# Gates of an RG-LRU recurrence: 64 by 64 quarters of the TensorE array in place of two 128 by 128 products per chunk

## The reference

```
xc = conv_b + causal convolution of xr over 4 tokens          # (T, 512)
xb = xc.reshape(B, T, N_RNN_BLOCKS, RNN_BLOCK)                # 8 blocks of 64 channels
r = sigmoid(einsum('btnc,ncd->btnd', xb, w_a) + b_a)
i = sigmoid(einsum('btnc,ncd->btnd', xb, w_i) + b_i)
log_a = -8 * r * softplus(-lam)
a = exp(log_a)
b = sqrt(-expm1(2 * log_a)) * i * xc
h = scan of  h[t] = a[t] * h[t-1] + b[t]
```

## Time and profile before

| | us |
|---|---|
| runs | 895.73, 898.94, 899.92; median 898.94 |
| profiled execution, its own time | 894.47 |
| its span, first to last instruction | 892.5 |
| TensorE, weight loads, VectorE, ScalarE busy | 861.2, 788.6, 683.0, 574.4 |
| gate stage of layer 0 (first gate product to the next query pair) | 51.79 to 55.98 |
| the same of layer 1 | 384.57 to 388.80 |

### The profile page before, as it was taken

The page is one execution under the profiler, slowest core; times in us unless marked ns, Lnnn a source line. Parts: engine busy times, 40 slices in busy tenths (PEclk is TensorE's granted clock), DMA queues, the critical chain, the costliest instruction groups (busy, mean ns, idle before and its releaser), DMA issues.

```text
span 892.5 us, 15446 instructions
## 1 busy us (share of the span) xinstructions
PE 861.2 (96%) x5827; PEld 788.6 (88%) x5827; DVE 683.0 (77%) x923; ACT 574.4 (64%) x792; POOL 70.8 (8%) x92
## 2 busy tenths in 40 slices
PE   8899999999999999899999999999999999999995
PEld 7856899999999999857899989999998989898994
DVE  5887876666665654877877989789887989789892
ACT  6686755545444534585656777777768777777772
POOL 3540110000000000000231000000000000000000
PEclk9999999999999999999999999999999999999998
DMA  9614034555576753314263999899998999899981
GB/s 312 194 48 144 21 123 147 190 183 188 182 212 183 201 154 107 95 49 142 71 213 118 341 353 371 303 356 400 339 395 295 382 370 363 301 364 391 347 355 26
DMA packets 119004, 208.18 MB, mean 233 GB/s; under 512 B 5920, under 2 KB 71712, under 8 KB 118944
## 3 DMA queue, kind: packets, MB, share of 16 engines
q1 hardware_dynamic: 117232, 201.79, 64.1%
q0 software_dynamic: 1424, 5.24, 2.9%
q10 hardware_dynamic: 288, 0.34, 0.2%
HBM read 202.12 MB, written 5.24 MB: 232 GB/s over the span
## 4 chain that ended last, share of the span: by engine, by line
PE 81%; DVE 10%; issue 3%; DMA 3%; ACT 2%; POOL 0%; ACTq 0%; DVEq 0%; SPq 0%; POOLq 0%
PE ps L2495 20%; PE ps L2520 13%; PE ps L652 11%; PE ps L654 11%; PE ps L653 11%; DVE wlo L1400 5%; PE ps L2097 2%; PE ps L2460 2%; PE ps L2213 1%; DMA raw<-in_moe_w_gate_dram 1%; ACT whi L958 1%; PE ps L2272 1%; DMA raw<-in_moe_w_down_dram 1%; PE ps L2116 1%; PE ps L2507 1%
## 5 line engine op out<-in xcount | busy, mean ns | idle before, releaser
L1400 DVE TENSOR_TENSOR wlo<-raw,whi 128x1536 fp32r<-128x1536 f32 (+4 forms) x298 | 437.8, 1494 | 91.0 <-ACT whi L958 87.8
L958 ACT ACTIVATE whi<-raw 128x1536 fp32r<-128x1536 f32 (+4 forms) x298 | 375.2, 1276 | 142.7 <-PE ps L654 75.6
L652 PE MATMUL ps<-uhi,whi 128*128 128x272 f32 (+1 forms) x576 | 169.2, 294 | 1.3 <-DVE ulo L1423 0.7
L654 PE MATMUL ps<-uhi,wlo 128*128 128x272 f32 (+1 forms) x576 | 165.9, 288 | 0.0
L653 PE MATMUL ps<-ulo,whi 128*128 128x272 f32 (+1 forms) x576 | 165.4, 287 | 0.0
L2495 PE MATMUL ps<-whi,xeh 128*128 128x320 f32 (+1 forms) x512 | 125.7, 326 | 0.0
L2495 PE MATMUL ps<-wlo,xeh 128*128 128x320 f32 (+1 forms) x512 | 124.3, 324 | 0.0
L2495 PE MATMUL ps<-whi,xel 128*128 128x320 f32 (+1 forms) x512 | 124.3, 324 | 0.0
L652 PEld LDWEIGHTS ps<-uhi,whi 128*128 128x128 f32 (+1 forms) x576 | 107.8, 187 | 5.1 <-issue 2.2
L653 PEld LDWEIGHTS ps<-ulo,whi 128*128 128x128 f32 (+1 forms) x576 | 108.0, 188 | 0.5
L654 PEld LDWEIGHTS ps<-uhi,wlo 128*128 128x128 f32 (+1 forms) x576 | 107.8, 187 | 0.0
(11 more groups left out here) (307 smaller groups left out, 1202.4 us busy)
## 6 DMA issues: line engine op xcount, KB each, us to landing
raw<-in_moe_w_down_dram SPq DMA_DIRECT2D x24, 1536.0 KB, 9.0
raw<-in_moe_w_gate_dram SPq DMA_DIRECT2D x16, 1536.0 KB, 7.8
raw<-in_moe_w_up_dram SPq DMA_DIRECT2D x16, 1536.0 KB, 8.3
raw<-in_moe_w_gate_dram SPq DMA_DIRECT2D x16, 1280.0 KB, 9.6
raw<-in_moe_w_up_dram SPq DMA_DIRECT2D x16, 1280.0 KB, 9.1
raw<-in_ffn_w_gate_dram SPq DMA_DIRECT2D x11, 1024.0 KB, 5.1
raw<-in_ffn_w_up_dram SPq DMA_DIRECT2D x11, 1024.0 KB, 5.2
raw<-in_ffn_w_down_dram SPq DMA_DIRECT2D x8, 1408.0 KB, 6.8
```

Of the source, the lines that this page charges most:

```text
L652: pe.matmul(dst, wh, xh, start=start, stop=False, skip_group_check=True)
L654: return pe.matmul(dst, wl, xh, start=False, stop=stop, skip_group_check=True)
L958: act.activation(placed(whi, s, src), src, ACT.Copy).then_inc(hi_done, 1)
L1400: dve.tensor_tensor(placed(wlo, s, src), src, placed(whi, s, src).bitcast(F32), ALU.subtract).then_inc(lo_done, 1)
```

## The change

TensorE works with quarters of its array. For each chunk it takes the two diagonal 64 by 64 matrices of `wa` and of `wi` alone: four products of 64 channels by 272 tokens, where `r` is the half of the channels and `at` the half of the PSUM partitions that takes the result. Half `s = 0` of the channels of both gates goes to the bank of `wa`, half `s = 1` of both to the bank of `wi`. In the first bank gate `wa` has partitions 0 to 63 and gate `wi` 64 to 127, in the second bank they are swapped, so that the four products of a chunk use four different quarters of the array. The list of blocks changes to `wa` 0, `wi` 0, `wa` 1, `wi` 1 and so on, so a chunk has banks 0 and 1 or banks 2 and 3. TensorE waits for both banks of a chunk, and both blocks count as filled together, after the fourth product.

A bank now holds half a chunk of two gates, so ScalarE empties it with two tanhs over 64 partitions, and there are 16 of them per layer. `decay_exp` begins with a new wait of ScalarE for its own mark after the tanhs.

```diff
--- before.py
+++ after.py
@@ -236,8 +236,8 @@
             add("qro", b)
         for j in range(2):
             add("qn", j)
-        for n in ("wa", "wi"):
-            for c in range(CH):
+        for c in range(CH):
+            for n in ("wa", "wi"):
                 add(n, c)
         for j in range(2, NH // 2):
             add("qn", j)
@@ -1079,19 +1079,22 @@
                 pairs("qn", qT, u32, range(2))
 
                 act.wait_ge(hba_done, 1)
-                for name, dst, bias in (("wa", ta, hba), ("wi", tb, hbi)):
-                    for c in range(CH):
-                        b = B[l, name, c]
-                        n = l * CH + c
+                for c in range(CH):
+                    n = l * CH + c
+                    for s, b in enumerate((B[l, "wa", c], B[l, "wi", c])):
+                        r = slice(64 * s, 64 * s + 64)
                         act.wait_ge(filled, b.ready())
-                        act.activation(dst[:, c, :], bank(b), ACT.Tanh, bias=bias[:, n:n + 1], scale=0.5)\
-                           .then_inc(emptied[b.bank], 1)
+                        for kind, (dst, bias) in enumerate(((ta, hba), (tb, hbi))):
+                            at = 64 * (kind ^ s)
+                            q = act.activation(dst[r, c, :], bank(b, slice(at, at + 64)), ACT.Tanh, bias=bias[r, n:n + 1], scale=0.5)
+                        q.then_inc(emptied[b.bank], 1)
                 mark().then_inc(ti_done, 1)
                 act.wait_ge(vec_done, 1)
                 act.wait_ge(xc_done, CH * (l + 1))
 
 
                 def decay_exp():
+                    act.wait_ge(ti_done, l + 1)
                     for c in range(CH):
                         n = l * CH + c
                         act.activation(xr[:, c, 0:T], ta[:, c, :], ACT.Exp, bias=nsp4[:, n:n + 1], scale=nsp4[:, n:n + 1])
@@ -2108,12 +2111,18 @@
                 query_pairs(range(2))
 
                 pe.wait_ge(gdiag_in, 64 * (l + 1))
-                for kind, name in enumerate(("wa", "wi")):
-                    for c in range(CH):
-                        b = B[l, name, c]
+                for c in range(CH):
+                    two = B[l, "wa", c], B[l, "wi", c]
+                    for b in two:
                         fill(pe, b)
-                        pe.wait_ge(xc_done, CH * l + c + 1)
-                        pe.matmul(bank(b), gdiag[:, kind, c, :], xc[:, c, :], start=True, stop=True).then_inc(filled, 1)
+                    pe.wait_ge(xc_done, CH * l + c + 1)
+                    for s, b in enumerate(two):
+                        r = slice(64 * s, 64 * s + 64)
+                        for kind in range(2):
+                            at = 64 * (kind ^ s)
+                            q = pe.matmul(bank(b, slice(at, at + 64)), gdiag[r, kind, c, r], xc[r, c, :], start=True, stop=True,
+                                          skip_group_check=True)
+                    q.then_inc(filled, 2)
                 query_pairs(range(2, NH // 2))
 
                 r = slice(NOPE, QKH)
```

## The result

The changed kernel takes 907.51 us (median of 5 runs, 905.16 to 908.73) against 898.94 (5 runs, 895.73 to 902.68). The ratio is 1.0098, with a 95% interval of 1.0073 to 1.0122: slower, by 8.6 us between the medians. The forecast was 907.2.

A forecast was written before the change was run, and what follows sets the result against it. TensorE and ScalarE were taken to bind side by side, ScalarE with 0.5 us slack. Tanhs +4.43 and wait +0.23, less slack, gave `rr` 4.15 us late per layer, +8.3 on 898.94: 907.2 us, range 901.5 to 911.0.

The forecast's parts named there:

- The step that carried the sum: ScalarE's gate tanhs: no overlap when the first partition changes, 0.50 us apart, run 7.99 us, +4.43 us per layer.
- only the reading side counts: Rival, gate tanhs: only a changed reading partition ends overlap; 3.25 us per layer, 905.4 us; chance 13%.
- the overlap stays: Rival, gate tanhs: starts stay 0.37 us apart; 2.1 us per layer, 903.1 us; chance 14%.
- The added wait: Ahead of decay_exp: waiting for ScalarE's own mark delays the exponentials, +0.23 us per layer.
- The slack: ScalarE up to `rr`: 0.35 us idle at the third key pair plus about 0.15 at `rr`, in all 0.5 us.
- TensorE's place in the wait: At the sums of squares ahead of `rr`: TensorE idles about 1.9 us until ScalarE's mark releases it.
- My 72.44 for L2184: Layer 0, TensorE's sums of squares: start shifts from 68.36 to 72.44 us, released by ScalarE's mark.
- TensorE's saving buys nothing: Gate stage: quarters save TensorE about 2 us, but a wait ahead of `rr` takes its place.
- No slack downstream: Behind `rr`: all is serial, so a late `rr` means a late end, one for one.
- Serial quarters: Rival, TensorE's gates: quarters run one after another, 1.03 us per layer more, 909.3 us; chance 8%.
- The rival that I gave 7%: TensorE's clock drops to half level, costing half of 3.4 us per layer, 910.6 us; chance 7%.

The follow-up runs named there:

- e1: The kernel before with nine groups of 272-column tanhs ahead of ScalarE's first work, differing in height and first partitions read and written; one run, 922.84 us.
- e7: The kernel before with only ScalarE's wait for its mark added ahead of decay_exp; one run, 897.65 us.
- e2: The kernel before with each gate bank emptied by two 64-row tanhs, lower then upper, and the mark's wait added; 903.95 us, ratio 1.0092.
- e4: The changed kernel's TensorE part, blocks and order, but 8 whole 128-row tanhs on ScalarE, mixing the gates' halves; 896.34 us, ratio 0.9989.
- e6: The changed kernel with three more 128 by 128 fp32 products per chunk behind the four quarters; 906.49 us, ratio 1.0084.
- e5: The changed kernel run again unaltered, to see where TensorE's clock falls; 905.94 us, ratio 1.0085.
- e8: The kernel before with squares and copies in pairs() reordered, so the first partition changes 2 times in two blocks instead of 4; one run, 897.49 us.

## Why the prediction was right

- **The overlap.** The step that carried the sum, 0.50 us between starts for every change of the first partition, measured 0.49 to 0.51 in layer 0 and 0.48 to 0.52 in layer 1, and 7.99 us for the run, as forecast. It was an inference from copies that change the reading side only. e1 shows that a change on the writing side (of the output or of the bias column, which moved together) counts too, so "only the reading side counts" and "the overlap stays" are out. The Trainium skill, ScalarE: Activation LUTs, What ACT_TABLE_LOAD costs, has back-to-back activations overlap by about 93 ns. e1 agrees where the first partition stays (0.11 us) and shows none where it changes.
- **The added wait** was put at 0.23 us; the exponentials now start 0.34 us behind the last tanh (61.35 to 61.69) where before they started 0.01 ahead, so 0.35. From mark to next start I took the 0.21 of a copy; to the exponentials it is 0.32 (61.37 to 61.69). In e7, where the mark still overlaps the last whole tanh by 0.1, the exponentials are 0.21 behind it.
- **The slack.** `rr` came 4.19 and 4.13 us late, forecast 4.15 for each. At `rr` the slack was 0.15 us, as I had it: from the root of `ta` to `rr` it is 1.15 us before (69.45 to 70.60) and 1.00 after (74.13 to 75.13). At the third key pair it was more than the idle 0.35 us, as the overlap of 0.11 comes back with it: from the squares ahead to the pair it is 0.76 us before and 0.29 after, 0.47 less. So 4.43 + 0.35 − 0.47 − 0.15 = 4.16. The wait and this slack were both taken 0.12 too small and cancel, which is luck.
- **TensorE's place in the wait** was wrong. I had it idle for 1.9 us at L2184 until ScalarE's mark. It starts L2184 without that, 1.91 us behind the start of the last value blocks (70.92 to 72.83), as in the kernel before (66.45 to 68.36), and waits ahead of these blocks for VectorE's rotation L1511, 0.48 us (1.14 in e2). VectorE works with no pause over 0.04 us from `decay_done`, ScalarE's second mark, up to that rotation, so this path is late together with ScalarE. With 2.24 us from L2184 to `rr` it is ready at 75.07, only 0.06 us before ScalarE. My 72.44 for L2184 (72.78 with the 0.34 us of this execution) hit by another path than the one I gave.
- **TensorE's saving buys nothing.** Shown twice: e4 gives 0.4 to 0.5 us per layer without the doubled tanhs, e6 adds 5.5 us of TensorE and loses 0.4. e2 has none of the saving and the same delay.
- **No slack downstream.** In e2, whose clock fell in the same stage as before's, VectorE's work is 4.3 us late after the gates and `rr` of layer 0 and 8.7 after those of layer 1, of which 0.2 and 0.3 came in ahead of the gates. Nothing was absorbed.
- **Serial quarters** are out: eight passes start within 0.30 us. The Trainium skill's sentence on four independent tiles (TensorEngine Tiling (Array Packing), Tiling Modes) holds here for fp32 and for both row groups.
- **The clock** fell in both gate stages of both profiles of the changed kernel; in the first, TensorE was at work for 1.51 of the 4 us ahead. The rival that I gave 7%, a fall ahead of L2184 at 1.7 us per layer, came in neither. A fall in the gates I had called hidden, without a chance for it: three of the four were, as ScalarE had more to do than TensorE even at half clock, and the fourth, 6.8 us long in e5, cost 0.54 us.
- **Against the right baseline** the match of 907.5 and 907.2 is closer than the method deserves: repeats of one kernel lie up to 8 us apart (894.66 to 902.58 for the kernel before, beside e1 to e4), and the same kernel gave 905.94 in e5.

## What to carry to other kernels

An instruction count on the engine that empties PSUM is a price of its own: halving a bank by partitions doubles it, because an activation costs by its columns (390 ns for 64x272, 397 for 128x272). Before taking work off the engine that the chain of waits names, read the timeline of the engine beside it for idle time, and take their sum (here 0.5 us, 0.6 with the overlap that comes back) as the most that can be gained. If activations have to work on parts of the partitions, order them so that first partitions on both sides change seldom.

## What the runs showed of the hardware that was not expected

- Consecutive activations overlapped by about 0.11 us only where neither the first partition read nor the one written changed: 0.37 us against 0.49 to 0.50 between starts for 272 columns with a bias column, whole height or half. Reading at 64 and writing at 0 throughout keeps the overlap. The bias column moved with the output in every run, so the two are not told apart.
- Thin work for TensorE (eight quarter passes in each 2 us) came with a fall of its clock to half in both gate stages in both profiles, and with full-size products in the gaps there was none (one profile). Other falls of 3.4 or 6.8 us (near 34, 85 to 89 and 480 us) came in some executions and not in others, before and after the change alike, and are worth up to 3.2 us each. They are a good part of the spread between repeats: of the 27 runs of the kernel before beside e1 to e8, the two with a mean granted clock of 0.986 took 900.8 and 902.6 us, the four with 0.995 took 894.7 to 896.7.
- A chain of tiny GpSimd operations off every chain in the first profile ended 0.5 us before its use, and in two of the later executions 1.5 us after the exponentials could have begun.
